# A hybrid encoder trunk: modulation in fp32 over four column quadrants, its panels spread over the gMLP heads, first projections between the tiles of h

## The reference

```
def modulate(x, c, norm_g, w_mod, b_mod):
    mod = jax.nn.silu(c) @ w_mod + b_mod
    shift, scale, gate = jnp.split(mod, 3, axis=-1)
    h = rms_norm(x, norm_g) * (1 + scale[:, None, :]) + shift[:, None, :]
    return h, gate[:, None, :]
...
    for l in range(DEPTH):
        h, gate = modulate(x, c, norm_g[l], w_mod[l], b_mod[l])
        ...
        x = x + gate * y
    return rms_norm(x, final_g), ...
```

## The kernel before

Main granules start only when half of h is ready:

```
                modulation_loops(pe, pair, layer)

                select(5, 1, True)

                pe.wait_ge(s["hT_done"], KT * layer + KT // 2)

                pe.wait_ge(s["h_done"], KT * (layer + 1))
```

## Time and profile before

| | us |
|---|---|
| median of 3 runs | 2930.8 |
| lowest, highest | 2925.21, 2931.32 |
| the profiled execution, its own time | 2932.06 |
| its span, first to last instruction | 2930.5 |

### The profile page before, as it was taken

The page is one execution under the profiler, slowest core; times in us unless marked ns, Lnnn a source line. Parts: engine busy times, 40 slices in busy tenths (PEclk is TensorE's granted clock), DMA queues, the critical chain, the costliest instruction groups (busy, mean ns, idle before and its releaser), DMA issues. The chain is left out here.

```text
span 2930.5 us, 40758 instructions
## 1 busy us (share of the span) xinstructions
PE 2811.0 (96%) x13344; PEld 2136.8 (73%) x13344; DVE 1484.1 (51%) x2013; ACT 1083.2 (37%) x1439; POOL 562.4 (19%) x669
## 2 busy tenths in 40 slices
PE   6689999999999999999989899999999999999997
PEld 2257778777888888888876577788777867787866
DVE  5775454545444554454446645454545444544544
ACT  5574332434233233233323644243344234332421
POOL 2030003100221111311113302122202320231123
PEclk9999999999999999999999999999999999999999
DMA  8876454656455555555545746554646454655454
GB/s 294 279 241 207 155 180 152 201 163 196 138 178 168 168 169 164 169 162 167 157 153 169 223 128 208 180 180 132 209 152 204 146 183 141 227 155 179 151 185 131
DMA packets 303013, 523.44 MB, mean 179 GB/s; under 512 B 33041, under 2 KB 131473, under 8 KB 301945
## 3 DMA queue, kind: packets, MB, share of 16 engines
q1 hardware_dynamic: 261570, 389.19, 42.1%
q0 software_dynamic: 41280, 132.20, 13.9%
HBM read 460.29 MB, written 60.96 MB: 178 GB/s over the span
## 5 line engine op out<-in xcount | busy, mean ns | idle before, releaser
L969 DVE TENSOR_TENSOR wlo<-raw,whi 128x1024 fp32r<-128x1024 f32 x733 | 900.3, 1242 | 975.3 <-ACT whi L672 971.7
L672 ACT ACTIVATE whi<-raw 128x1024 fp32r<-128x1024 f32 x733 | 769.0, 1057 | 1378.3 <-PE acc L1426 1274.7
L1426 PE MATMUL acc<-whi,hT_hi 128*128 128x512 f32 x2496 | 994.4, 398 | 2.0 <-DVE work L1086 1.2
L1426 PE MATMUL acc<-whi,hT_lo 128*128 128x512 f32 x2496 | 975.2, 391 | 0.0
L1426 PE MATMUL acc<-wlo,hT_hi 128*128 128x512 f32 x2496 | 974.8, 391 | 0.0
L1426 PEld LDWEIGHTS acc<-whi,hT_hi 128*128 128x128 f32 x2496 | 469.9, 188 | 138.3 <-issue 35.9
L1426 PEld LDWEIGHTS acc<-whi,hT_lo 128*128 128x128 f32 x2496 | 469.9, 188 | 100.4
L1426 PEld LDWEIGHTS acc<-wlo,hT_hi 128*128 128x128 f32 x2496 | 470.3, 188 | 94.5 <-issue 1.0
L1426 PE MATMUL acc<-whi,yT_hi 128*128 128x512 f32 x768 | 300.9, 392 | 3.5 <-DVE yT_lo L1095 2.6
L1426 PE MATMUL acc<-wlo,yT_hi 128*128 128x512 f32 x768 | 299.6, 390 | 0.0
L1426 PE MATMUL acc<-whi,yT_lo 128*128 128x512 f32 x768 | 299.5, 390 | 0.0
(11 more groups left out here) (200 smaller groups left out, 1980.2 us busy)
## 6 DMA issues: line engine op xcount, KB each, us to landing
raw<-in_w_in_e SPq DMA_DIRECT2D x448, 256.0 KB, 3.0
raw<-in_w_mod SPq DMA_DIRECT2D x384, 256.0 KB, 3.6
raw<-in_w_in_o SPq DMA_DIRECT2D x384, 256.0 KB, 3.1
out<-state POOLq DMA_DIRECT2D x96, 512.0 KB, 3.5
raw<-in_w_out_e SPq DMA_DIRECT2D x128, 256.0 KB, 3.4
state<-in_state_gla POOLq DMA_DIRECT2D x64, 512.0 KB, 5.2
raw<-in_w_out_o SPq DMA_DIRECT2D x128, 256.0 KB, 3.7
work<-gate_rows POOLq DMA_DIRECT2D x64, 256.0 KB, 4.5
```

What stands on the lines that cost most here:

```text
L672: act.activation(whi[jj][:, :, :], raw[jj][:, :, :], ACT.Copy).then_inc(s["hi_ready"], 1)
L969: dve.tensor_tensor(wlo[jj][:, :, :], raw[jj][:, :, :], whi[jj][:, :, :].bitcast(F32), ALU.subtract).then_inc(s["lo_ready"], 1)
L1426: return pe.matmul(out, lhsT, rhs, start=start, stop=stop, skip_group_check=True)
```

## The change

- **Modulation in fp32.** The modulation weights are not split any more and don't pass ACT and DVE. A panel is 4 batches (`batch`) of 4 k-tiles, 1 MB in two DMAs; each batch is four fp32 matmuls with `cT` (now plain silu(c) in 9 of 32 columns), the i-th into rows 32i to 32i+31 of one bank. Bias and norm_g come in transposed once (`vecT`), and `select` adds up the four row groups with a new `sel`; DVE adds the bias (`selected`).
- **Buffers.** The main stream of the gMLP part has only raw0 and raw2 (`load_main`, one DMA a granule); the batches have three pairs of buffers `MT`: raw1 with raw3, and the four `state` tiles, free until retention. SP waits for `mod_used` of the batch three before.
- **Order of the panels.** 24 panels in `PANEL`: the shift and scale panels of layer 0 run first, the other 16 in the gMLP heads and their output panels (`IN_HEAD`, `IN_OUT`), a batch after every second granule, two after every second granule in the last panel of head 0. The loops of this part are written out.
- **First projections.** In layer 0, granules 0 to 5 of head 0's first panel run between the batches and the tiles of h. In layer 1 modulation(1) is gone: `first_projection` turns the tiles of h and puts, from tile 3 on, after every second tile six matmuls of rank 16 and one granule. The gates of this head come after the projection, its diagonal scores and first levels two granules later. The x turns use the banks SC and OB[1].

```diff
+NBATCH = 4
+N_MOD = 24
+PANEL = [(0, q // 2 + 4 * (q % 2)) for q in range(8)] + [
+    (0, 8), (1, 0), (1, 1), (0, 9), (0, 10), (0, 11), (1, 8), (1, 9),
+    (1, 2), (1, 3), (1, 4), (1, 5), (1, 6), (1, 7), (1, 10), (1, 11)]
+IN_HEAD = [[[], [8], [9, 10]], [[11], [12], [13]], [[16], [17], [18]], [[19], [20], [21]]]
+IN_OUT = [[14, 15], [22, 23]]
...
+        MT = [(raw[1][:, :, :], raw[3][:, :, :])] + [
+            tuple(state[c][:, :].rearrange("p (k n) -> p k n", k=GK) for c in (2 * i, 2 * i + 1)) for i in range(2)]
...
+            def load_main(n, src):
+
+                at_least(sp, s["lo_ready"], n - 1)
+                sp.dma_start(raw[2 * (n % 2)][:, :, :], src).then_inc(main_in[n % 2], 16)
+
+            def load_batch(q, b):
+
+                layer, p = PANEL[q]
+                nb = BATCH[q, b]
+                at_least(sp, s["mod_used"], nb - len(MT) + 1)
+                for i in range(2):
+                    k = 4 * b + 2 * i
+                    sp.dma_start(MT[nb % len(MT)][i], w_m[layer][:, k:k + GK, p * W:p * W + W])\
+                        .then_inc(mod_in[nb % len(MT)], 16)
...
+            def panel_out(q):
+
+                act.wait_ge(s["mod_used"], BATCH[q, NBATCH - 1] + 1)
+                at_least(act, s["sel_full"], q)
+                act.activation(modsb, mod_bank(q)[:, :], ACT.Copy).then_inc(s["modsb_done"], 1)
...
+            def first_tiles(r):
+
+                act.wait_ge(s["x_added"], NT * O_GL + LEAD)
+                act.wait_ge(s["lrw_in"], 16)
+                act.activation(wlr[0], wlr_raw, ACT.Copy).then_inc(s["lrw_hi"], 1)
+                act.wait_ge(s["sel_done"], N_MOD)
+                for k in range(KT):
+                    prompt(1, k)
+                    if k:
+                        high(1, k - 1)
+                    if k % 2 and k >= 3:
+                        split(r + (k - 3) // 2 // NSLOT, (k - 3) // 2 % NSLOT)
+                high(1, KT - 1)
...
+            def batch(q, b):
+
+                nb = BATCH[q, b]
+                pe.wait_ge(mod_in[nb % len(MT)], 32 * (nb // len(MT)) + 32)
+                for i in range(4):
+                    ins = mm(mod_bank(q)[32 * i:32 * i + CROW, :], cT[:, 4 * b + i, :], MT[nb % len(MT)][i // 2][:, i % 2, :],
+                             b == 0, b == NBATCH - 1)
+                ins.then_inc(s["mod_used"], 1)
+
+            def select(q, dst):
+
+                pe.wait_ge(s["modsb_done"], q + 1)
+                at_least(pe, s["sel_done"], q)
+                if PANEL[q][1] >= 8:
+                    ins = mm(dst[0:NC9, :], sel[:, :], modsb)
+                else:
+                    for c in range(4):
+                        ins = mm(dst[:, NC9 * c:NC9 * c + NC9], modsb[:, P * c:P * c + P], sel[:, :])
+                ins.then_inc(s["sel_full"], 1)
...
+            def modulation():
                 pe.wait_ge(s["cT_done"], 1)
...
+                pe.wait_ge(s["vec_done"], 1)
+                for m in range(8):
+                    k0 = 4 * (m // 2 - 1)
+                    for b in range(NBATCH):
+                        if b == 0:
+
+                            at_least(pe, s["modsb_done"], m - 1)
+                        batch(m, b)
+                        if b == 0 and m:
+                            if m in (5, 7):
+                                pe.wait_ge(s["wsT_done"], m // 2 - 1)
+                            select(m - 1, OB[0])
+                        if m < 2:
+                            continue
+                        if m % 2 == 0 and b:
+                            turn_x(0, k0 + b - 1)
+                        if m % 2 and b == 0:
+                            turn_x(0, k0 + 3)
+                            va_main(m - 3)
+                        if m % 2 and b == 2:
+                            va_main(m - 2)
...
+            def gmlp(h, n0, ai, before):
...
+                for p in range(3):
+                    for g in range(6 if h + p == 0 else 0, 8):
+                        if h + p == 0:
+                            va_main(g)
+                        else:
+                            n = n0 + 8 * p + g
+                            granule(n, n % NSLOT, hT, GK * g, g == 0, g == 7, ai + p)
+                        if p == 0 and g == 0:
+
+                            at_least(pe, s["mix_done"], h * NT + LEAD)
+                        if g < len(before_panels(h, p)):
+                            select(before_panels(h, p)[g], SC)
...
+                        if g % 2:
+                            for q in IN_HEAD[h][p]:
+                                batch(q, g // 2)
...
             def ret_setup():
-                pe.wait_ge(s["mix_done"], NT * A_HEADS + LEAD)
+                select(N_MOD - 1, SC)
+                pe.wait_ge(s["sel_done"], N_MOD)
...
+            def first_projection(r, ai):
+
                 pe.wait_ge(s["lrw_done"], 1)
                 pe.wait_ge(s["o_done"], NT * B_HEADS + LEAD)
+
+                def part(g):
+                    pe.wait_ge(s["hT_done"], KT + GK * g + GK)
+                    for k in (2 * g, 2 * g + 1):
+                        for n, (hp, wp) in enumerate(((0, 0), (0, 1), (1, 0))):
+                            ins = mm(OB[0][0:RANK, 0:NTOK], wlr[wp][:, k, :], hT[hp][:, k, :],
+                                     k == 0 and n == 0, k == KT - 1 and n == 2)
+                    if g == 7:
+                        ins.then_inc(s["lrT_full"], 1)
+                    granule(4 * r + g, g % NSLOT, hT, GK * g, g == 0, g == 7, ai)
+
                 for k in range(KT):
...
+                    turn_x(1, k)
+                    if k % 2 and k >= 3:
+                        part((k - 3) // 2)
+                part(7)
```

More of the change, by code:

```diff
@@ L287, in walk @@
             out_panels("rt", 1, ("rt", 7, 8 + (Y_RT + 6), 6))
-            e["modulation"](1)
-            e["gla_setup"]()
             def mid_panels(ph):
@@ new lines, in gmlp, with gm_out @@
+                    split_main(n + 10)
+                    for q in IN_HEAD[h][p]:
+                        panel_out(q)
+            def gm_out(ph, pn, n, ai, yi, oi, before):
+                for g in range(4):
+                    split_main(n + g + 3)
+                    if g == 1 and before:
+                        turned(before, 0, True)
+                        turned(before, 2, True)
+                        act.wait_ge(s["va_out"], before[1] * 16 + 16)
+                if pn % 2:
+                    panel_out(IN_OUT[ph][pn // 2])
@@ new lines, in gm_out @@
+            def gm_out(ph, pn, n, ai, yi, oi, before):
+                for g in range(4):
+                    split_main(n + g + 3)
+                    if g == 0 and pn == 0:
+                        selected(IN_HEAD[2 * ph + 1][2][0], SC)
+                    if g == 0 and pn == 2:
+                        selected(IN_OUT[ph][0], T[0])
+                    if g == 1 and before:
+                        turned(before, 0, True)
+                        turned(before, 2, True)
+                panel_done("gm", ai, oi, 0, n + 3)
@@ L1350, in gla @@
                 last.then_inc(s["dif_done"], 1)
-                splits(r + 1)
+                if not first:
+                    splits(r + 1)
                 if mid:
@@ new lines, in gm_out @@
+            def gm_out(ph, pn, n, ai, yi, oi, before):
+                for g in range(NSLOT):
+                    granule(n + g, g, yT, GK * g, g == 0, g == NSLOT - 1, ai)
+                    if g == 0 and pn == 0:
+                        pe.wait_ge(s["mix_done"], (2 * ph + 2) * NT + LEAD)
+                        select(IN_HEAD[2 * ph + 1][2][0], SC)
+                    if g == 0 and pn == 2:
+                        select(IN_OUT[ph][0], T[0])
+                    if g == 1 and before:
+                        turn_out(before, 0, True)
+                        turn_out(before, 2, True)
+                        pe.wait_ge(s["yb_lo"], before[2] + 2)
+                    if g == 2 and before:
+                        turned(before)
+                    if g % 2:
+                        if g == 1 and pn == 0:
+                            pe.wait_ge(s["sel_done"], IN_HEAD[2 * ph + 1][2][0] + 1)
+                        batch(IN_OUT[ph][pn // 2], 2 * (pn % 2) + g // 2)
@@ L1840, in gla @@
                 project(r + 4, ai + 2, steps)
-            walk(pe, dict(start=start, modulation=modulation, gmlp=gmlp, ret_setup=ret_setup, ret=ret,
-                          gla_setup=gla_setup, gla=gla, out=out, finish=nothing))
+            walk(pe, dict(start=start, modulation=modulation, gmlp=gmlp, gm_out=gm_out, ret_setup=ret_setup, ret=ret, gla=gla,
+                          out=out, finish=nothing))
 def shape_constants():
```

858 lines of the change are left out of this document (420 added, 438 removed).

## The result

| | before | after |
|---|---|---|
| median, us | 2931.06 (4 runs, 2925.21 to 2932.74) | 2832.36 (4 runs, 2831.73 to 2834.97) |
| ratio to before | | 0.9669, interval 0.9656 to 0.9683 |
| span of the profiled execution, us | 2930.5 | 2831.2 |

The sign and the three places were right, two of the three sizes were not: the first stage gained 13 us more than forecast, and the heads lost 18 us less.

The account below looks back on a forecast made before the run. It took the first stage as bound by DMA, layer 1 by transfers and a four-engine chain, the rest by PE's queue. Gains of 81 and 26 us less a loss of 40 made 67 off 2930.8: 2864 us, range 2838 to 2900.

Parts of the forecast that it names:

- The sign: Whole kernel: faster than before, at 0.94; same (under 0.2%, 6 us) 0.02, slower 0.04.
- the three places: Where time would change: first stage (DMA bytes), gMLP heads (PE time), layer 1 (chain latency).
- the three sizes: First stage 81 us gained, gMLP heads 40 us lost, layer 1 26 us gained.
- Step 1: First stage: 40.1 MB at 280 GB/s, 143 us, PE's work hidden; gain 81 us (65 to 93).
- Step 2: gMLP heads and output panels: added batches, entries and selects outweigh removed modulation granules; loss 40 us (21 to 60).
- Step 3: Retention heads: unchanged at 759 us.
- Step 4: Layer 1: second projection 31 us earlier, then stalls of 2.7 and 2.3 us from late gates; gain 26 us (12 to 36).
- D: First stage and heads: 310 GB/s and batches of 1.05 us, more gain than forecast, 2835 us; chance 0.06.
- A: First stage and layer 1: PE stays at 1.2 GHz, +25 and +30 us, about 2919, half of it 2891; chance 0.13.
- B: gMLP heads: SP's issue order makes main weights late in panel z and behind double waits, 2888 us; chance 0.09.
- C: Heads and first stage: quadrants don't overlap, a batch costs 3.4 us, 3043 us; decides from 2.0 us a batch; chance 0.04.
- E: gMLP heads: the gates' panels return as PE stalls, 67 us over 64 batches, nothing gained, 2931 us; chance 0.02.

Follow-up runs that it names:

- small_dmas: The changed kernel with each modulation batch in four DMAs of 256 KB and each gMLP main granule in two, in place of 512 KB each; 2835.1 us.
- apart: The changed kernel with one granule a panel in the first stage, behind the panel's third batch, and granule 5 behind the last batch, on PE alone; 2823.9 us.
- four_buffers: The changed kernel with a fourth pair of buffers for the 32 batches of the first stage; 2821.7 us.
- two_buffers: The changed kernel with two pairs of 1 MB buffers for the batches in place of three; 2879.0 us.
- before_early_turned: The kernel before, with ACT and DVE taking the turned tiles of y after the seventh and ninth split in each round's second gMLP head; 2923.0 us against 2929.8.
- late_turned: The changed kernel with ACT and DVE taking both pairs of turned tiles of y behind the sixth split, not the fourth and fifth; 2844.4 us.
- high_in_pairs: The changed kernel with ACT making the high halves of two layer-1 tiles together behind the prompt of each odd tile; 2821.4 us.
- double_batch: The changed kernel with each batch's four matmuls issued twice and the stationary values halved, so only PE's work grows; 2895.0 us.
- one_quadrant: The changed kernel with a modulation panel's sixteen k-tiles added up in rows 0 to 31, one matmul after the other, not in four row groups; 3035.3 us.

## Why the prediction was right and wrong

**Step 1, first stage: wrong, +13 us.** The step that failed is "At 280 GB/s that is 143 us". I took a rate off the kernel before and called it the DMA's. The slices of after pass at up to 410 on the same queue, and small_dmas shows that the size of a DMA isn't the limit. What held the kernel before at 280 is not shown; its four buffers of 0.5 MB, which come free only after the splits by ACT and DVE, are the likely reason (see small_dmas). The Trainium skill (DMA: Bandwidth & Descriptors, Where 436 GB/s comes from) gives about 358 GB/s per core for loads from HBM and 435 as the ceiling of the fabric; the 408 held over 12 us in after, on one busy core, are above the first and under the second. My sentence "freed by PE alone, so I expect no lower rate" named the right mechanism and stopped short: with three buffers the stage was bound neither by the DMA's rate nor by PE's sum, but by PE's longest stretches between batches (apart, four_buffers, two_buffers). The last batch was at 135.4 in place of 145, and at 129.7 to 132.6 in the five other traces of the same stage. Granule 6 took 4.2 us, not 6.5: its matmuls start every 0.23 us from the second on, after a wait of 2.12 us; those at the low clock in this stage are in the granules 0, 2 and 4 (5.7 to 6.1 us each to the batch behind).

**Step 2, heads: wrong, 18 us too dear.** The batch at 1.0 us was right. Entering was mis-sized: 60 entries at 0.2 are 12 us where I had 18. And "Turns of y, mixing and their waits stay" was wrong: in the changed kernel `turned` stands behind the fourth and fifth split, in the code before behind the eighth of the mixed stream. That is 8 us in the traces (twice 2.4 of waiting and 1.7 at the low clock behind it) and 6.8 by before_early_turned, and standing behind the sixth split it would have cost 12 (late_turned). These two make 14 of the 18; the last select (1.7 in place of 2.5) is a small part, and some 3 us are spread over the batches and granules and were not followed. The Trainium skill (TensorEngine Tiling (Array Packing), Key Properties) says that a change of mode drains TensorE; 0.2 us per batch is all that could be seen of it.

**Step 3** was right (759.6).

**Step 4, layer 1: right in the sum, not in its parts.** First turn 8.5 us after the last granule (forecast "some 8"), period 8.20 (8.45), the second projection 35.6 us earlier (31), and ACT's order as the reason is shown by high_in_pairs. The stall was 7.8 us where I had 5 in two waits, and at another place: not the fourth granule's split but the third turn, which waits for ACT's copy of the first; from the second projection on the loss was 9.2 in all. I had listed the splits behind the exponentials and not the copies, though they stand in the same queue between them. Two errors of 5 and 4 us with opposite signs left the 26 right, which is luck.

**Rivals.** D had nearly the right time (2835), and its higher rate is there. Its other half, 16 us from batches of 1.05 us with their entries, is not: they cost 1.2, and the heads came out 18 us cheaper mainly by the turns of y. A is there in part: the low clock shows in the first stage (0.81) and behind each wait, but six traces of the same stage with mean clocks from 0.81 to 0.90 differ by 5 us only. B is real (two_buffers), yet absent with three buffers. C has its size now, 203 us, and its condition did not hold. E did not happen: no wait of PE in the heads is left over but 2.8 us.

## What to carry over

A rate of transfer in a stage is the DMA's only if nothing holds its buffers. So first multiply the bytes of the buffers by how often they come free, and compare with the highest slice of the same trace. With a few buffers between a queue and an engine, what counts is the longest stretch in which the engine frees none, so spread the engine's other work evenly, or add a buffer; do both, and the engine's own work becomes the bound. And when a loop is written anew, each wait in it is priced anew, together with the low clock behind it: the place of two copies in a queue was worth 7 to 12 us here.

## What the hardware showed that I had not expected

- Loads from HBM ran at 400 to 412 GB/s for 11 us and longer, in DMAs of 512 KB (after) and of 256 KB (small_dmas).
- A wait of TensorE cost nearly twice its length. Behind 2.42 us of idle time (before) and 3.40 us (late_turned) the granted clock was 0.50, and the granule that followed took about 2 us longer.
- More work for PE in a stage with gaps cost next to nothing: 32 more passes over a batch took 4 to 8 us (double_batch), and the mean clock up to 135 us was 0.95 in place of 0.81. With 3.55 us batches it was 1.00 from 20 us on (one_quadrant). Work with gaps ran partly at 1.2 GHz: a batch took 1.87 us at 43.2 us in after, at a granted clock of 0.50, and 1.0 later.
- Four fp32 matmuls of 32 stationary columns take 3.55 us one behind the other and 1.0 us in four row groups; a second pass over the same weights costs 0.88.
